# Routing each token tile beside the output projection, and the second layer's modulation ahead of its use

## The chip, the cores and the metric

The kernel runs on one core of one Trainium2 chip. The metric is the device time of one execution, in microseconds (us). The kernel before took 2386.52 us as the median of three runs (2384.01 to 2393.23).

## The reference

Two layers over 512 latent and 256 context tokens of width 1024, all in float32. The first layer mixes tokens with gated DeltaNet and grouped attention heads, the second with neighbourhood attention; each layer ends in an expert-choice mixture of 16 experts. What matters here is the end of each layer:

```python
h = h + mod_l[2] * y_lat                       # y_lat = heads @ w_out
h = h + mod_l[5] * expert_choice_ffn(modulate(h, ln2_g[layer], mod_l[3], mod_l[4]), *moe)
# modulate(x, g, shift, scale) = rms_norm(x, g) * (1 + scale) + shift
def expert_choice_ffn(h, w_router, w_gate, w_up, w_down):
    cap = max(1, EC_CAPACITY * t // N_EXPERTS)
    aff = jax.nn.softmax((h @ w_router).astype(F32), axis=-1)
    gate, idx = lax.top_k(jnp.swapaxes(aff, 1, 2), cap)
    xs = jax.vmap(lambda hb, ib: hb[ib])(h, idx)
    hid = silu(xs @ w_gate) * (xs @ w_up)
    y = (hid @ w_down) * gate                  # scattered back to the tokens and added
```

Each of the 16 experts picks its 64 best latent tokens (and 32 context tokens in the first layer, where the context goes through the same weights). The choice needs the logits of all tokens; so nothing of an expert can start before the last tile of the output projection has been normalised and multiplied by the router.

## The kernel before, in words

Tokens lie in tiles of 128: two of context, four of latents. Each engine runs a program of its own, written out by hand; semaphores join them, and every engine takes its instructions in the written order. The stages around the change are these.

- **Output projection** (outproj0_pe in the first layer, outproj_pe in the second; outproj_dve on VectorE). TensorE makes one half tile (128 tokens by 512 columns) after the other, 8 blocks of weights each; a half has the number j, two halves are a tile. VectorE multiplies half j with the modulation's gate (L1838) while it adds half j-1 to the residual stream H (L1846). Four PSUM banks let TensorE run four halves ahead. Of the first four halves of the first layer, half of the products are made earlier. The first layer has 12 halves, the second 8.
- **Second normalisation and router** (norm_act, norm_dve, norm_pe, logits_pe, pick_pe, pick_dve). ScalarE squares each tile of H as it is finished and takes one root over all; VectorE scales all tiles (L378); TensorE turns them (L403), VectorE and ScalarE modulate what was turned (L390, L364), TensorE multiplies with the router (L1912) and turns back (L1929), VectorE sums four groups (L1974) and takes the maximum (L1975), the softmax, and eight rounds of max / find / replace. The last small steps copy the token numbers out of PSUM (L2018, TOKL; L2021, TOKC; L2031), and GpSimd gathers the tokens of the first pair of experts (L2328, L2330); TensorE turns them (L2138, L2142), VectorE and ScalarE modulate (L2244, L2218).
- **Experts** (moe_pe and others). Pairs of experts, 24 MB of weights to a pair, streamed by SyncE into 8 or 12 slots that are full before the first pair starts; each slot is loaded again when its products are done.
- **Between the layers** the last pair's sums go back to the tokens (last_back, L2165, with the additions L2262), then TensorE turns the second layer's modulation rows (ada_finish_pe, L256), spreads the gates (ada_gates_pe, L279, copied by ScalarE L287), and the first normalisation of the second layer follows.

The order of work is the order of the code.

## Time and profile before

| what | value |
|---|---|
| median of the runs | 2386.52 us (2384.01 to 2393.23) |
| the profiled execution, first to last instruction | 2382.3 us |
| TensorE busy | 2112.3 us, 89% |
| VectorE busy | 762.8 us, 32% |
| ScalarE busy | 447.2 us, 19% |
| mean granted TensorE clock | 0.935 |

Shares are averages over stages that have different limits. The profile's busy time of TensorE holds modelled ends of pipelined matmuls; a float32 matmul shows as two records, a transpose as one. The chain of waits follows the work that ended last back through the program; a difference in a stage that is not on it is worth nothing.

### The profile page before, as it was taken

What the parts mean: (1) busy time and instruction counts of PE and PEld (TensorE: products, weight loads), DVE (VectorE), ACT (ScalarE), POOL (GpSimd) and SP (SyncE); (2) the same over time, 40 slices, a digit from 0 to 9 for tenths busy, and PEclk for the clock granted to TensorE, in tenths of its full rate; (3) what the DMA queues carried; (4) which work ended last, traced back from release to release, by engine and by line L of the source; (5) the groups of instructions that cost most, each with busy time, mean ns of one, the idle gap of its engine ahead of it and who ended that gap; (6) DMA issues with size and microseconds to landing.
All of it is one profiled execution on the core that took longest, in us unless ns stands there. A gap on an engine that the chain in (4) does not pass through costs nothing.

```text
span 2382.3 us, 32937 instructions
## 1 busy us (share of the span) xinstructions
PE 2112.3 (89%) x13760; PEld 1076.7 (45%) x13760; DVE 762.8 (32%) x1384; ACT 447.2 (19%) x1008; POOL 121.9 (5%) x119
## 2 busy tenths in 40 slices
PE   5998999818689849999999989999999399999997
PEld 3544666517685413333333334554674144444442
DVE  2143523588874341011011113000681511111113
ACT  2213421575321110000000012000561000000001
POOL 0000000030110000011111000000000000000000
PEclk9999999857679969999999999999999699999999
DMA  7219730132125339999999982210313399999996
GB/s 285 71 64 345 248 130 13 38 95 84 63 77 200 113 126 378 398 395 399 390 398 395 401 343 77 60 44 1 111 41 134 132 408 421 421 421 421 421 421 276
DMA packets 110618, 551.30 MB, mean 231 GB/s; under 512 B 13024, under 2 KB 25824, under 8 KB 61328
## 3 DMA queue, kind: packets, MB, share of 16 engines
q1 hardware_dynamic: 102512, 522.29, 55.6%
q0 software_dynamic: 7168, 23.83, 3.5%
q10 hardware_dynamic: 800, 3.15, 0.3%
q8 instruction: 111, 1.82, 0.3%
q14 instruction: 27, 0.22, 0.0%
HBM read 525.27 MB, written 22.38 MB: 230 GB/s over the span
## 4 chain that ended last, share of the span: by engine, by line
PE 75%; DMA 11%; DVE 9%; ACT 2%; issue 2%; SPq 0%; POOL 0%; DVEq 0%; POOLq 0%; ACTq 0%
PE ps L2104 22%; PE ps L2114 5%; DMA ring_sb<-expert_w_up 5%; PE ps L498 5%; PE ps L1789 3%; PE ps L901 3%; PE ps L2468 3%; PE ps L1821 2%; PE ps L2440 2%; PE ps L2449 2%; PE ps L2132 2%; DMA ring_sb<-ada_w 2%; PE ps L2151 2%; PE ps L900 2%; PE ps L244 2%
## 5 line engine op out<-in xcount | busy, mean ns | idle before, releaser
L2104 PE MATMUL ps<-work_sb 128*32 128x512 f32 (+1 forms) x2432 | 408.1, 593 | 9.6 <-ACT work_sb L2235 5.5
L2104 PE MATMUL ps<-ring_sb,work_sb 128*32 128x512 f32 (+1 forms) x2048 | 300.5, 599 | 16.6 <-DMA ring_sb<-expert_w_up 9.8
L2104 PEld LDWEIGHTS ps<-work_sb 128*32 128x32 f32 (+1 forms) x2432 | 123.0, 120 | 231.5 <-issue 224.2
L2104 PEld LDWEIGHTS ps<-ring_sb,work_sb 128*32 128x32 f32 (+1 forms) x2048 | 87.8, 118 | 204.3 <-issue 198.1
L2291 DVE TENSOR_TENSOR work_sb<-ps,work_sb 128x512 f32<-128x512 f32 x32 | 20.6, 687 | 437.1 <-PE ps L2114 329.8
L2225 ACT ACTIVATE work_sb<-ps 128x1024 f32<-128x1024 f32 x16 | 16.4, 1024 | 515.9 <-PE ps L2114 295.8
L498 PE MATMUL ps<-ring_sb,work_sb 128*128 128x512 f32 (+1 forms) x288 | 109.2, 541 | 0.9 <-DVE work_sb L390 0.9
L2114 PE MATMUL ps<-work_sb 128*32 128x512 f32 x768 | 100.7, 592 | 0.0
L2114 PE MATMUL ps<-ring_sb,work_sb 128*32 128x512 f32 x768 | 100.4, 593 | 0.0
L901 PE MATMUL ps<-work_sb,ring_sb 128*128 128x512 f32 x192 | 98.0, 592 | 0.0
L2310 DVE SCALAR_TENSOR_TENSOR work_sb<-ps,work_sb,gates_sb 128x1024 f32<-128x1024 f32 x16 | 20.5, 1284 | 232.9 <-PE ps L2114 124.8
L2235 ACT COPY work_sb<-ps 128x512 f32<-128x512 f32 x32 | 17.3, 589 | 405.7 <-PE ps L2192 405.7
L244 PE MATMUL ps<-ring_sb,sT_sb 128*32 128x512 f32 x384 | 57.0, 692 | 30.0 <-DMA ring_sb<-ada_w 28.2
L1789 PE MATMUL ps<-ring_sb,work_sb 128*128 128x512 f32 x192 | 82.8, 592 | 0.0
L498 PEld LDWEIGHTS ps<-ring_sb,work_sb 128*128 128x128 f32 x288 | 55.6, 194 | 52.4 <-issue 46.2
L2253 DVE TENSOR_TENSOR h_sb<-ps,h_sb 128x512 f32<-128x512 f32 x64 | 42.5, 688 | 100.2 <-PE ps L2151 100.2
L2468 PE MATMUL ps<-ring_sb,work_sb 128*128 128x512 f32 x160 | 68.8, 592 | 0.0
L2244 DVE TENSOR_SCALAR work_sb<-ps,scaleT_sb,modT_sb 128x128 f32<-128x128 f32 x128 | 42.2, 403 | 82.5 <-PE ps L2132 65.0
L2449 PE MATMUL ps<-work_sb,ring_sb 128*128 128x512 f32 x128 | 65.4, 592 | 0.0
L784 DVE TENSOR_REDUCE work_sb<-ps 128x1 f32<-128x768 f32 (+1 forms) x48 | 35.2, 775 | 78.5 <-PE ps L708 78.5
L2151 PE MATMUL ps<-work_sb 128*128 128x512 f32 x128 | 58.9, 604 | 1.5 <-DVE work_sb L2310 1.5
L2104 PE MATMUL ps<-h_sb,work_sb 128*64 128x512 f32 x128 | 57.6, 592 | 0.6 <-DMA work_sb<-expert_w_down 0.6
(405 smaller groups left out, 2913.2 us busy)
## 6 DMA issues: line engine op xcount, KB each, us to landing
work_sb<-expert_w_down SPq DMA_DIRECT2D x88, 1024.0 KB, 17.4
work_sb<-expert_w_gate SPq DMA_DIRECT2D x64, 1024.0 KB, 9.5
ring_sb<-expert_w_gate SPq DMA_DIRECT2D x64, 1024.0 KB, 10.0
ring_sb<-expert_w_up SPq DMA_DIRECT2D x64, 1024.0 KB, 13.9
work_sb<-expert_w_up SPq DMA_DIRECT2D x56, 1024.0 KB, 14.6
...
```

The source lines that it names most:

```text
L244: mm = pe.matmul(ps[32 * q:32 * q + 32, bank, :], sT[:, k, :], w[:, a * 512:(a + 1) * 512], start=(k == 0), stop=(k == KT - 1))
L498: mm = pe.matmul(ps[:, j % 4, 0:N], A[:, k, tok_cols(tt):tok_cols(tt) + P], w[:, (k % 2) * N:(k % 2 + 1) * N], start=(k == 0), stop=(k == ...
L900: pe.matmul(ps[:, b + 1, 0:CTX], w[:, k, :], A[:, k, 0:CTX], start=(k == 0), stop=(k == KT - 1))
L901: mm = pe.matmul(ps[:, b, :], w[:, k, :], A[:, k, LO:LO + LAT], start=(k == 0), stop=(k == KT - 1))
L1789: mm = pe.matmul(ps[:, EVEN_BANKS[j % 4], :], YT[:, tt, k, :], w[:, half * 512:half * 512 + 512], start=(k == 0), stop=(k == KT - 1))
L1821: mm = pe.matmul(ps[:, 4 + j % 4, :], c(k), w[:, half * 512:half * 512 + 512], start=(k == 0), stop=(k == KT - 1))
L2104: mm = pe.matmul(ps[g:g + wide, bank + n, :], lat_src[:, k, g:g + wide], us[e][:, n * 512:(n + 1) * 512], start=(k == 0), stop=(k == KT - 1))
L2114: mm = pe.matmul(ps[g:g + 32, bank_c, :], ctx_src(k, e), us[e][:, n * 512:(n + 1) * 512], start=(k == 0), stop=(k == KT - 1))
L2132: mm = pe.matmul(ps[:, k // 4, k % 4 * P:(k % 4 + 1) * P], XM[:, CT + j, cols(k)], TAKE[:, p % 2, j, :], start=(j == 0), stop=(j == LT - 1))
L2151: pe.matmul(ps[:, 4 + g % 4, :], ONEHOT[:, j * P:(j + 1) * P], YL[l][:, half * 512:half * 512 + 512], start=True, stop=True).then_inc(h_mm, 1)
L2449: mm = pe.matmul(ps[:, b, :], w[:, k, :], AO[:, k, LO:LO + LAT], start=(k == 0), stop=(k == KT - 1))
L2468: mm = pe.matmul(ps[:, 2 * (i % 2) + side, :], AO[:, k, v_cols(m):v_cols(m) + P], w, start=(k == 0), stop=(k == KT - 1))
```

## The change

- The router no longer works on normalised tiles. A raw tile of H is turned as soon as it is added up (route_turn_pe), copied out of PSUM in two halves by VectorE (route_dve) and ScalarE (route_act), and multiplied by router weights that hold the modulation's scale (WRM, router_weights_dve); the root of the tile and the product of shift and router (CVEC) come in afterwards (route_logits_dve). Each tile's steps are written between the halves of the output projection (route_beside_pe); route_end_pe has what is left.
- VectorE adds half j right behind its multiplication, where before it added half j-1.
- The second layer's modulation is turned after half 1 of the first layer's output projection; its gates are spread during the first layer's choice of tokens; only two gates are made instead of four. The tables of both layers are kept.
- The first normalisation of the second layer goes tile by tile between the last additions of the experts' sums (norm_row_dve).
- Normalised rows are stored tile by tile; the first gather waits for TOKL alone, the second (context) for TOKC, and the first products for half of the modulated tokens.
- GpSimd loads SEL1 and the router's weights (WR) right behind the late half of H (x); in the second layer WR goes ahead of the final gain.

On TensorE, first layer, from the first four half products on, before; L1789 are products of the output projection (8 to a half), L1761 turns of the heads' output, L403 turns of the normalised tiles:

```order
L1789 MATMUL ps<-ring_sb,work_sb 128x512 x16
L1761 MATMUL ps<-base_sb,h_sb 128x128 x16
L1789 MATMUL ps<-ring_sb,work_sb 128x512 x80
L403 MATMUL ps<-base_sb,work_sb 128x128 x36
L1912 MATMUL ps<-work_sb 32x512 x4
L1912 MATMUL ps<-work_sb 32x256 x4
```

and now, from half 2 on; L1798 is the projection, L1898 the turn of a raw tile, L1916 the spread of the shift's product, L1931 the logits of a tile, L1937 their turn back:

```order
L1798 MATMUL ps<-ring_sb,work_sb 128x512 x4
L1898 MATMUL ps<-base_sb,h_sb 128x128 x8
L1798 MATMUL ps<-ring_sb,work_sb 128x512 x4
L1916 MATMUL ps<-work_sb,base_sb 128x16 x2
L1931 MATMUL ps<-work_sb 32x128 x8
L1798 MATMUL ps<-ring_sb,work_sb 128x512 x8
L1937 MATMUL ps<-base_sb,work_sb 128x128
L1898 MATMUL ps<-base_sb,h_sb 128x128 x8
L1798 MATMUL ps<-ring_sb,work_sb 128x512 x8
L1931 MATMUL ps<-work_sb 32x128 x8
L1798 MATMUL ps<-ring_sb,work_sb 128x512 x8
```

Behind every odd half from 3 on now stand the logits of a tile, behind every even half from 4 on a turn back and the turn of the next tile.

On VectorE, same place, halves 6 and 7, with the semaphores that each instruction waits for; L1851 is the gate's multiplication, L1857 the addition, L2016 and L2005 copies out of PSUM, L2023 the sum of groups, L2007 and L2009 the inverse root and the normalised tile:

```order
L1851 TENSOR_TENSOR work_sb<-ps,gates_sb 128x512 [waits op_mm]
L1857 TENSOR_TENSOR h_sb<-h_sb,work_sb 128x512 [waits h_late,op_ok]
L2016 COPY work_sb<-ps 128x128 [waits rl_mm]
L1851 TENSOR_TENSOR work_sb<-ps,gates_sb 128x512 [waits op_mm]
L1857 TENSOR_TENSOR h_sb<-h_sb,work_sb 128x512 [waits h_late,op_ok]
L2023 TENSOR_REDUCE work_sb<-ps 128x16 [waits rl_mm]
L2025 SCALAR_TENSOR_TENSOR work_sb<-work_sb,stats_sb 128x16 [waits lg_ok]
L2005 COPY work_sb<-ps 128x512 [waits rl_mm,rt_mm]
L2007 RECIPROCAL stats_sb<-stats_sb 128x1 [waits rt_ok]
L2009 TENSOR_SCALAR work_sb<-h_sb,stats_sb 128x1024 [waits rc_ok]
```

The copies that TensorE's new instructions need stand behind the multiplication and the addition of the same half; before, only L1838 and L1846 stood here.

The diff, cut to its core:

```diff
                 else:
                     pe.wait_ge(op_ok, j - 3)
                     half_products(j, turned + list(range(4, KT)))
+                route_beside_pe(pe, 0, j)
+            route_end_pe(pe, 0)
...
-        def outproj_dve(dve, u0, tiles, mm_sem, prod_sem, ok_sem, w, PROD, base=0, banks=(4, 5, 6, 7)):
+                route_beside_pe(pe, 1, j)
+            route_end_pe(pe, 1)
+
+        def outproj_dve(dve, l, u0, mm_sem, prod_sem, ok_sem, PROD, banks=(4, 5, 6, 7)):
+            tiles, base = routed_tiles(l), OP0 * l
...
+            for j in range(n):
+                tt, half = tiles[j // 2], j % 2
+                if j < n - 1:
+                    dve.wait_ge(mm_sem, max(base - 1, 0) + j + 1)
+                else:
+                    dve.wait_ge(w_free, u0 + KT)
+                v = 1 if tt < CT else 0
+                nc.vector.tensor_tensor(PROD[:, j % 4, :], ps[:, banks[j % 4], :], gate_at(l, 0, v)[:, half * 512:half * 512 + 512],
+                                        ALU.mult).then_inc(ok_sem, 1)
+                dve.wait_ge(ok_sem, base + j + 1)
+                if l == 0:
+                    dve.wait_ge(h_back if tt < CT else h_late, 16)
+                hh = H[:, tt, half * 512:half * 512 + 512]
+                nc.vector.tensor_tensor(hh, hh, PROD[:, j % 4, :], ALU.add).then_inc(prod_sem, 1)
+                if j == 1 and l == 0:
+                    ada_finish_dve(dve, 1, (0, 1))
+                if j == 2:
+                    router_weights_dve(dve, l)
+                if j % 2 == 0 and j >= 4:
+                    route_sums_dve(dve, l, j // 2 - 2)
+                if j % 2 == 1 and j >= 5:
+                    route_logits_dve(dve, l, (j - 5) // 2)
+                if j % 2 == 1 and j >= 3:
+                    route_dve(dve, l, (j - 3) // 2)
+            last = len(tiles) - 1
+            route_sums_dve(dve, l, last - 1)
+            route_dve(dve, l, last)
+            route_logits_dve(dve, l, last - 1)
+            route_sums_dve(dve, l, last)
+            route_logits_dve(dve, l, last)
...
+        def route_turn_pe(pe, l, n):
+
+            tt = routed_tiles(l)[n]
+            pe.wait_ge(op_x, OP0 * l + 2 * n + 2)
+            if n == 0 and l == 0:
+                pe.wait_ge(modT_ok, 5)
+            if n > 0:
+                pe.wait_ge(rt_dve, NT * l + n)
+                pe.wait_ge(rt_act, NT * l + n)
+            for k in range(KT):
+                tr = pe.transpose(ps[:, TURN_BANKS[l][k // 4], k % 4 * P:(k % 4 + 1) * P], H[:, tt, cols(k)], IDENT)
+                if k % 4 == 3:
+                    tr.then_inc(rt_mm, 1)
+
+        def route_shift_pe(pe, l):
+
+            if l == 0:
+                pe.wait_ge(yt_ok, NT)
+            pe.wait_ge(mo["wr"], 16 * (l + 1))
+            pe.wait_ge(modT_ok, MODULATED["n2_%d" % l])
+            for k in range(KT):
+                mm = pe.matmul(ps[0:2, LOGIT_BANK[l], P:P + NE], MOD[:, l, :, 3, k], WR[:, k, :], start=(k == 0), stop=(k == KT - 1))
+            mm.then_inc(rl_mm, 1)
+
...
+        def route_logits_pe(pe, l, n):
+
+            tt = routed_tiles(l)[n]
+            if n > 0:
+                pe.wait_ge(rl_ok, logits_ok(l, 2 * n + 1))
+            for half in range(2):
+                pe.wait_ge((rt_dve, rt_act)[half], NT * l + n + 1)
+                for j in range(4):
+                    k = 4 * half + j
+                    w = WRM[:, 1 if tt < CT else 0, k, :]
+                    w = bass.AP(w.tensor, w.offset, [w.ap[0], [1, 32]])
+                    mm = pe.matmul(ps[32 * j:32 * j + 32, LOGIT_BANK[l], 0:P], w, RT[:, k, :], start=(half == 0), stop=(half == 1))
+            mm.then_inc(rl_mm, 1)
+
+        def route_back_pe(pe, l, n):
+
+            pe.wait_ge(rl_ok, logits_ok(l, 2 * n + 3))
+            pe.transpose(ps[:, BACK_BANK[l], 0:P], TURNED, IDENT).then_inc(rl_mm, 1)
...
+        def route_beside_pe(pe, l, j):
+
+            if j == 1:
+                route_shift_pe(pe, l)
+                if l == 0:
+                    ada_finish_pe(pe, 1, (0, 1))
+            if j >= 4 and j % 2 == 0:
+                route_back_pe(pe, l, j // 2 - 2)
+            if j >= 2 and j % 2 == 0:
+                route_turn_pe(pe, l, j // 2 - 1)
+            if j == 3:
+                route_spread_pe(pe, l)
+            if j >= 3 and j % 2 == 1:
+                route_logits_pe(pe, l, (j - 3) // 2)
+
+        def route_end_pe(pe, l):
+            last = len(routed_tiles(l)) - 1
+            route_back_pe(pe, l, last - 1)
+            route_turn_pe(pe, l, last)
+            route_logits_pe(pe, l, last)
+            route_back_pe(pe, l, last)
+
+        def route_act(act, l):
+            root_table(act)
+            for n, tt in enumerate(routed_tiles(l)):
+                act.wait_ge(op_x, OP0 * l + 2 * n + 2)
+                if n >= 2:
+                    act.wait_ge(sq_ok, tiles_before(l) + n - 1)
+                nc.scalar.activation(MJ[:, n % 2, :], H[:, tt, :], ACT.Square, accum_out=stat_t[:, tt:tt + 1]).then_inc(sq_ok, 1)
+                act.wait_ge(rt_mm, 2 * (NT * l + n) + 2)
+                if n > 0:
+                    act.wait_ge(rl_mm, logits_mm(l, 2 * n + 1))
+                nc.scalar.copy(RT[:, 4:8, :].rearrange("p k t -> p (k t)"), ps[:, TURN_BANKS[l][1], :]).then_inc(rt_act, 1)
+                act.wait_ge(sq_ok, tiles_before(l) + n + 1)
+                nc.scalar.activation(stat_t[:, 8 + tt:9 + tt], stat_t[:, tt:tt + 1], ACT.Sqrt, bias=EPSC, scale=1.0 / D) \
+                    .then_inc(rt_ok, 1)
+
...
+        def route_dve(dve, l, n):
+
+            tt = routed_tiles(l)[n]
+            dve.wait_ge(rt_mm, 2 * (NT * l + n) + 1)
+            if n > 0:
+                dve.wait_ge(rl_mm, logits_mm(l, 2 * n + 1))
+            nc.vector.tensor_copy(RT[:, 0:4, :].rearrange("p k t -> p (k t)"), ps[:, TURN_BANKS[l][0], :]).then_inc(rt_dve, 1)
+            dve.wait_ge(rt_ok, tile_roots_before(l) + n + 1)
+            nc.vector.reciprocal(stat_t[:, 16 + tt:17 + tt], stat_t[:, 8 + tt:9 + tt]).then_inc(rc_ok, 1)
+            dve.wait_ge(rc_ok, tile_roots_before(l) + n + 1)
+            nc.vector.tensor_scalar(XM[:, tt, :], H[:, tt, :], stat_t[:, 16 + tt:17 + tt], None, ALU.mult).then_inc(xn_ok, 1)
+
+        def route_sums_dve(dve, l, n):
+
+            dve.wait_ge(rl_mm, logits_mm(l, 2 * n + 3))
+            if n == 0:
+                nc.vector.tensor_copy(CVEC.rearrange("p v e -> p (v e)"), ps[:, BACK_BANK[l], P:P + 2 * NE]).then_inc(rl_ok, 1)
+            nc.vector.tensor_copy(TURNED, ps[:, LOGIT_BANK[l], 0:P]).then_inc(rl_ok, 1)
+
+        def route_logits_dve(dve, l, n):
+
+            tt = routed_tiles(l)[n]
+            dve.wait_ge(rl_mm, logits_mm(l, 2 * n + 4))
+            groups = ps[:, BACK_BANK[l], 0:P].rearrange("p (j e) -> p e j", j=4)[:, 0:NE, :]
+            nc.vector.tensor_reduce(LG[:, tt, :], groups, AX, ALU.add).then_inc(lg_ok, 1)
+            dve.wait_ge(lg_ok, NT * l + n + 1)
+            nc.vector.scalar_tensor_tensor(AFF[:, tt, :], LG[:, tt, :], stat_t[:, 16 + tt:17 + tt],
+                                           CVEC[:, 1 if tt < CT else 0, :], ALU.mult, ALU.add).then_inc(rl_ok, 1)
...
             tr.then_inc(mo["aft"], 1)
+            if l == 0:
+                ada_gates_pe(pe, 1)
             pe.wait_ge(mo["sid"], 2 * l + 2)
             n = C0 + NE if l == 0 else NE
...
             for e in range(2):
                 r = slice(CAP_L * e, CAP_L * e + CAP_L)
+                last = nc.vector.tensor_copy(TOKL[r, :], ps[r, 4, e:NE:2])
+            last.then_inc(mo["sg"], 1)
+            if l == 0:
+                for e in range(2):
+                    r = slice(CAP_C * e, CAP_C * e + CAP_C)
+                    last = nc.vector.tensor_copy(TOKC[r, :], ps[r, 4, C0 + e:C0 + NE:2])
+                last.then_inc(mo["sg"], 1)
+            for e in range(2):
+                r = slice(CAP_L * e, CAP_L * e + CAP_L)
                 if l == 1:
...
                     if l == 0:
+                        if m == 0 and k == 0:
+                            pe.wait_ge(mp["xsc"], p + 1)
                         if m == 2 and k == 0:
...
-                    last = nc.vector.tensor_scalar(XP[:, k, :], ps[:, k // 4, k % 4 * P:(k % 4 + 1) * P],
-                                                   AT[:, 1, 0, k:k + 1], modT[:, 0, 3, k:k + 1], ALU.mult, ALU.add)
-                last.then_inc(mp["xs"], 1)
+                    last = nc.vector.tensor_scalar(XP[:, k, :], ps[:, TOKEN_BANK[l] + k // 4, k % 4 * P:(k % 4 + 1) * P],
+                                                   SCALE[:, l, 1, 0, k:k + 1], MOD[:, l, 0, 3, k:k + 1], ALU.mult, ALU.add)
+                    if k % 4 == 3:
+                        last.then_inc(mp["xs"], 1)
...
                     hh = H[:, tt, half * 512:half * 512 + 512]
                     nc.vector.tensor_tensor(hh, ps[:, BACK_BANKS[g % 4], :], hh, ALU.add).then_inc(h_add, 1)
+                    if half == 1 and g >= 3:
+                        norm_row_dve(dve, "n1_1", g // 2 - 1, LATENTS_FIRST[g // 2 - 1], XNO)
 
...
             def gather(p):
                 pool.indirect_dma_start(XG, None, xm_rows, at(TOKL[:, p:p + 1])).then_inc(mp["got"], 16)
                 if l == 0:
-                    pool.indirect_dma_start(XGC[0:64], None, xm_rows, at(TOKC[0:64, p:p + 1])).then_inc(mp["got"], 16)
+                    if p == 0:
+                        pool.wait_ge(mo["sg"], 2)
+                    pool.indirect_dma_start(XGC[0:64], None, xm_rows, at(TOKC[0:64, p:p + 1])).then_inc(mp["gotc"], 16)
...
             pool.dma_start(H[:, CT:NT, :], t["x"].rearrange("(t p) d -> p t d", p=P)).then_inc(h_late, 16)
-            pool.wait_ge(gate_ok, 4)
-            pool.wait_ge(w_free, U_MOE[0])
+            pool.wait_ge(dn_ok, len(ORDER))
+            pool.dma_start(SEL1, t["sel"].rearrange("p (s m) -> p s m", s=8)).then_inc(ada1_in, 16)
             pool.dma_start(WR, t["router"][0].rearrange("p (k e) -> p k e", k=KT)).then_inc(mo["wr"], 16)
             moe_pool(pool, 0)
             odd_pool(pool)
             pool.wait_ge(op_mm, OP0)
+            pool.dma_start(WR, t["router"][1].rearrange("p (k e) -> p k e", k=KT)).then_inc(mo["wr"], 16)
             pool.dma_start(FING, t["fin_g"].partition_broadcast(P)).then_inc(fin_in, 16)
-            pool.dma_start(WR, t["router"][1].rearrange("p (k e) -> p k e", k=KT)).then_inc(mo["wr"], 16)
             moe_pool(pool, 1)
```

## Rows read from the trace of the kernel before

**Rows 1.** Page, part 4: the chain that ended last, by engine.
```profile
PE 75%; DMA 11%; DVE 9%; ACT 2%; issue 2%; SPq 0%; POOL 0%; DVEq 0%; POOLq 0%; ACTq 0%
```
**Rows 2.** Chain in order of time: start us, us, what.
```profile
749.37 68.68 PE ps L1789 x160
...
867.59 5.87 DMA work_sb<-xm_rows,work_sb
...
1889.80 4.35 DMA work_sb<-xm_rows,work_sb
```
**Rows 3.** Timeline, VectorE: start us, us, engine line operation, count [idle before <-releaser].
```profile
818.08 0.69 DVE L1838 TENSOR_TENSOR work_sb<-ps,gates_sb 128x512 f32<-128x512 f32 x1 [5.58 <-PE ps L1789]
818.69 1.70 DVE L1846 TENSOR_TENSOR h_sb<-h_sb,work_sb 128x512 f32<-128x512 f32 x2
...
841.20 0.25 DVE L1975 TENSOR_REDUCE work_sb<-work_sb 128x6 f32<-128x96 f32 x1
...
863.72 0.15 DVE L2018 CAST work_sb<-ps 64x8 uint32<-64x8 f32 x1
...
865.25 0.17 DVE L2031 TENSOR_SCALAR work_sb<-ps 64x16 uint32<-64x16 f32 x1
875.59 2.64 DVE L2244 TENSOR_SCALAR work_sb<-ps,scaleT_sb,modT_sb 128x128 f32<-128x128 f32 x8 [10.18 <-PE ps L2138]
...
1437.32 3.40 DVE L378 TENSOR_SCALAR work_sb<-h_sb,stats_sb 128x1024 f32<-128x1024 f32 x5
1441.56 0.75 DVE L378 TENSOR_SCALAR work_sb<-h_sb,stats_sb 128x1024 f32<-128x1024 f32 x1 [0.84 <-PE ps L279]
...
1867.80 0.22 DVE L1975 TENSOR_REDUCE work_sb<-work_sb 128x4 f32<-128x64 f32 x1
```
**Rows 4.** Groups of instructions by form, VectorE: a copy of 128 columns out of PSUM.
```profile
L535 DVE COPY work_sb<-ps 128x128 f32<-128x128 f32 x6 | 1.8, 292 | 20.7 <-PE ps L498 20.7
```
**Rows 5.** Timeline, TensorE, several stretches.
```profile
112.33 0.59 PE L593 MATMUL ps<-work_sb 128*128 128x8 f32 x4
112.77 0.37 PE L594 MATMUL ps<-work_sb,base_sb 128*128 128x16 f32 x2
...
747.46 1.91 PE L1761 MATMUL ps<-base_sb,h_sb 128*128 128x128 f32 x16
...
833.57 1.50 PE L1912 MATMUL ps<-work_sb 128*32 128x512 f32 x16
...
879.31 3.64 PE L2104 MATMUL ps<-ring_sb,work_sb 128*32 128x512 f32 x16 [2.61 <-issue]
...
1421.30 12.23 PE L2165 MATMUL ps<-work_sb 128*128 128x512 f32 x24 [2.24 <-DVE work_sb L2316]
...
1442.37 1.70 PE L403 MATMUL ps<-base_sb,work_sb 128*128 128x128 f32 x12 [0.85 <-DVE work_sb L378]
...
1794.12 55.20 PE L1821 MATMUL ps<-ring_sb,work_sb 128*128 128x512 f32 x128 [1.73 <-DVE work_sb L2588]
```
**Rows 6.** Timeline, GpSimd: its DMA issues.
```profile
749.68 0.78 POOL L2872 DMA_DIRECT2D h_sb<-x  x1 [18.16 <-PE ps L1761]
...
866.25 1.04 POOL L2328 DMA_INDIRECT work_sb<-xm_rows,work_sb  x1 [44.05 <-DVE work_sb L2031]
```
**Rows 7.** DMA issues: count, KB each, median us from issue to landing.
```profile
h_sb<-x POOLq DMA_DIRECT2D x1, 2048.0 KB, 8.7
```
**Rows 8.** Timeline, ScalarE.
```profile
820.42 1.06 ACT L351 ACTIVATE work_sb<-h_sb 128x1024 f32<-128x1024 f32 x1 [6.73 <-DVE h_sb L1846]
...
876.73 2.48 ACT L2218 ACTIVATE work_sb<-ps,modT_sb,scaleT_sb 128x64 f32<-128x64 f32 x8 [12.42 <-PE ps L2142]
```
**Rows 9.** Windows: stretch, us, PE, PEld, DVE, ACT, POOL busy (count), clock, DMA share, GB/s.
```profile
1419.00:1421.00 2.00, 0.07 (x4) 0.00 (x0) 1.78 (x2) 0.00 (x0) 0.00 (x0) 1.00 0.52 80
1422.00:1424.00 2.00, 2.00 (x4) 0.75 (x3) 0.69 (x1) 0.00 (x0) 0.00 (x0) 0.60 1.00 393
1794.00:1796.00 2.00, 1.89 (x5) 0.93 (x6) 0.06 (x1) 0.51 (x2) 0.00 (x0) 1.00 0.00 0
```

297 lines of the change are left out of this document (131 added, 166 removed).

## The prediction

> **What bounds the kernel now.** I read the chain of waits first: 75% of it is TensorE, 11% DMA, 9% VectorE [rows 1]. So a microsecond of TensorE's stream in a stage that is on the chain is a microsecond of the kernel. The chain in order of time then says which stages those are: in the first layer's output projection it is TensorE alone for 68.68 us, without one piece of another engine between, up to 818.05 [rows 2]. The timeline of VectorE says what it does meanwhile: it waits 5.58 us of every half for TensorE, and its own multiplication and addition are 0.69 and 0.68 us [rows 3]. The reader is to see here that VectorE has room in the projection, TensorE has none. Behind the projection it is turned round: the maximum over the logits starts at 841.20, 23.15 us after the last product, and in the second layer at 1867.80, 18.5 us after 1794.12 + 55.20 = 1849.3 [rows 3, 5]. These two tails are what the change can shorten. The choice of tokens that follows (841.20 to 863.6) is untouched.
>
> **Part 1: the tails.** What is left behind the last half, e being the moment at which VectorE sees it done: multiplication and addition 1.4 us [rows 3]; group sum and combination of the tile before, 0.2 each (near the 0.25 of a small reduce [rows 3]), and the copy of 512 columns (0.7, as long as the multiplication): e + 2.45. Logits on TensorE to e + 3.6, the copy of 128 columns 0.29 [rows 4], the turn back, the last tile's turn (8 of 1.91 / 16 = 0.12, with latency 1.2): e + 5.4. ScalarE's copy and root on the last tile, beginning behind that turn, end at e + 6.4, its square (1.06 [rows 8]) is long done. Inverse and normalised tile on VectorE (0.2 + 0.68), which stand ahead of the sums: e + 7.35. Two sums, a combination, one copy and a turn back: e + 8.8. So the maximum starts 8.8 us behind the last half in place of 23.15 and 18.5: **-14.3 and -9.7 us**. ScalarE's change of tables for the exponential comes behind its last root and is hidden by VectorE's 2.4 us there; bare it would be another 1.3.
>
> **Part 2: what is put between the halves.** The order of the changed program decides this one. Behind odd half j TensorE has the logits of a tile, and they wait for a copy that VectorE makes only after multiplying and adding half j itself. Behind an even half TensorE has a turn back, which waits for a copy that again follows the multiplication and the addition of the same half. VectorE cannot begin these before TensorE has finished the half, and behind TensorE's waiting instruction stand the 8 products of the next half, which wait with it. The four banks ahead are worth nothing then. Price of a wait: odd, 1.4 + 0.4 + 0.7 = 2.45 us (2.05 for j = 3, where no sums stand ahead), even, 1.4 + 0.29 = 1.7 us. A restart adds 0.16: a product occupies 0.43 (68.68 / 160) and its end is seen after 0.59, so one overlap is lost.
>
> TensorE's own work: a turn of a tile 1.0 (8 x 0.12 [rows 5]), a turn back 0.15. The logits of a tile are 8 float32 matmuls, 16 records; with the same weights and longer rows 16 (L1912) took 1.50 us [rows 5], by columns alone they would be 0.4. I take 1.0, keep 0.4 and 1.6. The product of shift and router is 16 records of tiny matmuls, at (112.77 - 112.33) / 4 = 0.11 [rows 5] 1.8 us; its weights are two columns wide, I take 1.5, keep 1.0 and 1.8. The turn of the modulation rows, 8 turns, is 1.0.
>
> One more wait, first layer only: the product of shift and router needs WR. GpSimd issues the load of H at 749.68, which lands 8.7 us later, at 758.4 [rows 6, 7]; SEL1 (512 KB) and WR (64 KB) are issued behind it on the same queue. At the rate of that load (2048 KB in 8.7) they need up to 2.4 more, at the engines' full rate 1.4: WR lands near 760. Half 1 is done at 818.05 less eight halves of 6.87 and two of 3.43, that is 756.2. Wait 3.8 us; keep 0 (WR overtakes) and 5.
>
> First layer, halves 1 to 10: WR 3.8 + 1.5 + 1.0; turn 1.0; j = 3: 2.05 + 0.16 + 1.0 = 3.2; j = 5, 7, 9: 3.6 each, 10.8; j = 4, 6, 8, 10: 1.7 + 0.16 + 0.15 + 1.0 = 3.0 each, 12.0. Sum **+33.3**. Second layer (WR is loaded a whole half earlier), halves 1 to 6: 1.5 + 1.0 + 3.2 + 3.6 + 2 x 3.0 = **+15.3**.
>
> **Part 3: the first gather.** Only TOKL is awaited now: two copies of 0.15 from 863.6 on, in place of everything up to 865.42 [rows 3]; GpSimd's issue moves from 866.25 to 864.7. A lone gather took 4.35 us from its issue in the second layer; in the first two of them and SEL1 took from 866.25 to 867.59 + 5.87 = 873.5 [rows 2, 6]. The latents' tokens now don't wait for the context's: landed by 869.2, turned by 871.2, half modulated (half of 2.64 [rows 3]) by 872.6, where the first product of experts came at 879.31 [rows 5]. The context's tokens, ready at about 875.7 with ScalarE's 2.48 [rows 8], are needed after the latents' first products, 3.64 us at that clock. **-6.3**, keep -4 and -7. In the second layer one reordered copy, **-0.5**.
>
> **Part 4: between the layers.** Before, the last normalised tile was done at 1442.3, for its last scale waited for the gates' products (L378) [rows 3]. Now VectorE has 12 additions of 0.69, six inverses and scales of 0.2 + 0.68 and small zeroings of about 1 us: some 14.6 us from about 1422.5 (1421.30 [rows 5] and a slow first product), plus 1.5 in the slow start, 1438.6. TensorE has then been idle for 5 us and turns the first columns slowly, 0.5. **-3.2**, keep -1 and -5. Two copies of gates and eight records of gate products move under the 22 us of the token choice, where TensorE and ScalarE wait anyway; without that cover they would be 3.4 us.
>
> **Part 5: TensorE's clock.** After 2.24 us of idleness [rows 5] the granted clock fell from 1.00 to 0.60 of the next two microseconds, between 2.4 and 1.2 GHz [rows 9]; after 1.73 idle at the start of the second projection it stayed at 1.00 [rows 5, 9]. The long waits here are 2.45, followed by thin logits, the short ones 1.7. In the first case 24 products took 12.23 where 24 x 0.43 = 10.3 would do, about 1.7 more (VectorE's additions share in that). I take such a fall for half of the six odd waits, none for the even: **+5**, keep 0 and 20.
>
> The Trainium skill, "TensorE: Matmul & The Clock Gate", section "HAM oscillation — how this bites in real kernels", has the clock fall only after idleness longer than any wait counted here; by it this term is 0 and the sum 5 us less. Row 9's fall after 2.24 us disagrees, so the row goes into the sum.
>
> **The sum.** 33.3 - 14.3 - 6.3 = +12.7 in the first layer; -3.2 between; 15.3 - 9.7 - 0.5 = +5.1 in the second; clock +5: +19.6 us. A late start of the experts passes on whole: their slots are full before they start in both kernels and are refilled only as they are used. The profiled execution spans 2382.3 us, 4.2 less than the runs' median of 2386.5; so 2382.3 + 19.6 + 4.2 = **2406 us**. Its own range, by the bounds above, is 2395 to 2421.
>
> **Rivals.**
> - *The hand-overs cost nothing* (faster). If VectorE's copies were always ready when TensorE asks, 12 waits with restarts (26.0), the wait for WR (3.8) and the clock's 5 go: 2406 - 34.8 = 2371. For it speaks that VectorE is idle for 5.58 us of each half; against it, that this idleness lies before the end of the half, and the copies are written behind it. It decides from the point where the 12 waits, 2.2 us on average with their restarts, fall to 0.95: then the clock stays up too (-5), and the other 14.6 us of the sum are gone. Chance 0.07.
> - *Part of it is cheaper*: logits at 0.4, WR in time, no fall of the clock: 2406 - 3.6 - 3.8 - 5 = 2394, no difference that can be told. Chance 0.2.
> - *The clock falls at nearly every wait*: nine more falls of 1.7 us: 2421. For it, the thin matmuls behind each wait; against it, the even waits' length, which cost nothing before the second projection. Chance 0.15.
> - *The change doesn't reach the end*: the weight stream absorbs the late starts. DMA is 11% of the chain. Then only the transition is left, 2383. Against it, that the stream itself stands still until products free its slots. Chance 0.05.
> - The forecast: 0.5. Mishaps of no name, 0.03.
>
> Within 0.5% (11.9 us) a measurement of this kernel can hardly tell a difference; so faster is below 2374.6, slower above 2398.5. Faster 0.07, same 0.22 (the second rival, the fourth, and a little of the forecast's low end), slower 0.71. The range that leaves out 2 in 10 is 2387 to 2422.
>
> **What would show it.** In the changed profile: TensorE waits for VectorE's copy at L2005 behind odd halves, 2.0 to 2.5 us each, and for the copy at L2016 behind even ones, 1.5 to 1.9; the first projection's products end 33 us later after their start than before, the second's 15; the maximum (L2115) starts 8 to 10 us behind the last product; a wait of 3 to 5 us for WR at L1909 in the first layer only; the first expert products about 10 us after the chosen tokens are turned. If the waits at L1931 and L1937 are below 1 us, the step on hand-overs is wrong, and with it the sign.

## The result and the profile after

The changed kernel takes 2404.8 us as the median of four runs (2401.48 to 2411.64), the kernel before 2387.06 in four runs on the same chip (2384.01 to 2393.23). The ratio is 1.0085, with a 95% interval of 1.0062 to 1.0109: slower by 0.85%. The profiled execution spans 2399.7 us, 17.4 more than that of before; its mean granted clock is the same 0.935. One of the runs below, the sixth of the second experiment, took 3191.03 us at a mean granted clock of 0.659, a slower state of the chip, and is left out of that experiment's median. The page's chain by engine hardly differs from that of before [rows 1], so it can't say where the time went:

```profile
PE 74%; DMA 11%; DVE 10%; ACT 2%; issue 2%; SPq 1%; POOL 0%; DVEq 0%; POOLq 0%; ACTq 0%
```

The stages can. Their bounds are starts of TensorE's groups in the two timelines, except the end of each projection, which is the start of the next group less the wait printed for it.

| stage | before | after | difference |
|---|---|---|---|
| up to the second loop of the first projection | 749.37 | 744.52 | -4.9 |
| first projection to its last product | 68.7 | 104.6 | **+35.9** |
| to the first product of the experts | 61.3 | 40.7 | **-20.6** |
| experts, to the first product of the last sums | 542.0 | 545.5 | +3.5 |
| between the layers, to the mixer's first product | 31.3 | 26.5 | **-4.8** |
| the second layer's mixer | 341.5 | 340.6 | -0.9 |
| second projection | 55.2 | 70.8 | **+15.6** |
| to the first product of its experts | 49.7 | 39.7 | **-10.0** |
| to the end | 483.3 | 486.9 | +3.5 |

The difference of the first stage is not the change's: it took 744.2 to 749.8 us in ten profiles of changed kernels (this one and nine below) and 748.4 in a second profile of the kernel before. In the first projection the products of the halves used to run without a gap [rows 2]. Now TensorE's timeline (start us, us, engine line operation, count, and in brackets how long the engine was idle before and whom it waited for) reads so:

```profile
755.06 0.59 PE L1909 MATMUL ps<-work_sb,modT_sb 128*2 128x16 f32 x16 [3.51 <-issue]
755.58 1.98 PE L256 MATMUL ps<-base_sb,modrows_sb 128*128 128x128 f32 x8
...
765.63 0.61 PE L1916 MATMUL ps<-work_sb,base_sb 2*128 2x16 f32 x4
767.81 0.65 PE L1931 MATMUL ps<-work_sb 128*32 128x128 f32 x16 [1.57 <-DVE work_sb L2005]
768.39 8.77 PE L1798 MATMUL ps<-ring_sb,work_sb 128*128 128x512 f32 x16
778.98 0.33 PE L1937 MATMUL ps<-base_sb,work_sb 128*128 128x128 f32 x1 [1.81 <-DVE work_sb L2016]
...
780.11 7.03 PE L1798 MATMUL ps<-ring_sb,work_sb 128*128 128x512 f32 x16
789.75 0.65 PE L1931 MATMUL ps<-work_sb 128*32 128x128 f32 x16 [2.61 <-DVE work_sb L2005]
790.32 7.13 PE L1798 MATMUL ps<-ring_sb,work_sb 128*128 128x512 f32 x16
...
830.14 1.08 PE L1931 MATMUL ps<-work_sb 128*32 128x128 f32 x16 [2.61 <-DVE work_sb L2005]
831.15 8.12 PE L1798 MATMUL ps<-ring_sb,work_sb 128*128 128x512 f32 x16
...
851.75 0.65 PE L1931 MATMUL ps<-work_sb 128*32 128x128 f32 x16 [2.61 <-DVE work_sb L2005]
852.80 0.33 PE L1937 MATMUL ps<-base_sb,work_sb 128*128 128x128 f32 x1 [0.40 <-DVE work_sb L2016]
...
854.50 1.20 PE L1931 MATMUL ps<-work_sb 128*32 128x128 f32 x16
```

L1931 are the logits of a tile, L1937 is the turn back of the logits' sums, L1798 a half (7.03 us are its 8 products, 16 records, at full clock; 8.77 and 8.12 are halves that began at the lower one), L1898 the turn of a raw tile. All the waits are there that the prediction named. VectorE's timeline at 787 to 790 shows who is waited for:

```profile
787.18 0.69 DVE L1851 TENSOR_TENSOR work_sb<-ps,gates_sb 128x512 f32<-128x512 f32 x1 [8.26 <-PE ps L1798]
787.90 0.69 DVE L1857 TENSOR_TENSOR h_sb<-h_sb,work_sb 128x512 f32<-128x512 f32 x1
788.51 0.22 DVE L2023 TENSOR_REDUCE work_sb<-ps 128x16 f32<-128x64 f32 x1
788.77 0.24 DVE L2025 SCALAR_TENSOR_TENSOR work_sb<-work_sb,stats_sb 128x16 f32<-128x16 f32 x1
788.92 0.69 DVE L2005 COPY work_sb<-ps 128x512 f32<-128x512 f32 x1
```

VectorE idled 8.26 us until the half was done; the copy L2005 that TensorE waits for is the fifth instruction in its queue behind that moment, and ends at 789.61, 0.14 us before TensorE goes on. The idleness of VectorE is real, and it lies on the wrong side of the additions.

The tails are short now. The maximum over the logits, L2115, which stood at 841.20 and 1867.80 before [rows 3]:

```profile
1881.92 0.22 DVE L2115 TENSOR_REDUCE work_sb<-work_sb 128x4 f32<-128x64 f32 x1
```

In the first layer it starts at 857.88, 8.7 us behind the last product (849.14); here 8.75 behind 1873.17.

### The profile page after: what moved, and what is told of

Its sections match the earlier page's. It is cut to its first block, busy times and chain, and to the rows that moved or that the text cites. A ratio compares the mean times of both kernels' runs of the same rounds, so it can differ in the third digit from the quotient of the medians.

```text
span 2399.7 us, 33292 instructions
## 1 busy us (share of the span) xinstructions
PE 2119.6 (88%) x13904; PEld 1077.9 (45%) x13904; DVE 765.0 (32%) x1425; ACT 449.1 (19%) x1020; POOL 121.2 (5%) x119
## 3 DMA queue, kind: packets, MB, share of 16 engines
q1 hardware_dynamic: 102512, 522.29, 55.2%
## 4 chain that ended last, share of the span: by engine, by line
PE 74%; DMA 11%; DVE 10%; ACT 2%; issue 2%; SPq 1%; POOL 0%; DVEq 0%; POOLq 0%; ACTq 0%
PE ps L2258 22%; PE ps L2270 5%; PE ps L508 4%; DMA ring_sb<-expert_w_up 4%; PE ps L1798 4%; PE ps L911 3%; DMA work_sb<-expert_w_up 3%; PE ps L2628 3%; PE ps L1832 2%; PE ps L2600 2%; PE ps L2609 2%; PE ps L2288 2%; DMA ring_sb<-ada_w 2%; PE ps L2308 2%; PE ps L910 2%
## 5 line engine op out<-in xcount | busy, mean ns | idle before, releaser
L2449 DVE TENSOR_TENSOR work_sb<-ps,work_sb 128x512 f32<-128x512 f32 x32 | 20.6, 687 | 440.0 <-PE ps L2270 331.0
L1798 PE MATMUL ps<-ring_sb,work_sb 128*128 128x512 f32 x192 | 89.6, 621 | 0.0
L2628 PE MATMUL ps<-ring_sb,work_sb 128*128 128x512 f32 x160 | 68.8, 592 | 0.0
L1832 PE MATMUL ps<-ring_sb,work_sb 128*128 128x512 f32 x128 | 57.5, 603 | 1.7 <-DVE work_sb L2748 1.7
```

The source lines that it names most:

```text
L1798: mm = pe.matmul(ps[:, EVEN_BANKS[j % 4], :], YT[:, tt, k, :], w[:, half * 512:half * 512 + 512], start=(k == 0), stop=(k == KT - 1))
L1832: mm = pe.matmul(ps[:, 4 + j % 4, :], c(k), w[:, half * 512:half * 512 + 512], start=(k == 0), stop=(k == KT - 1))
L2628: mm = pe.matmul(ps[:, 2 * (i % 2) + side, :], AO[:, k, v_cols(m):v_cols(m) + P], w, start=(k == 0), stop=(k == KT - 1))
```

## The experiments

Ten runs follow: eight edits of the changed kernel, and the kernel before and the changed one once more. Line numbers in a fence are those of the kernel that it shows; an edit moves some of them by up to 8.

**VectorE's router work ahead of the additions.** VectorE's part of the router beside half j is issued at the top of the turn of the loop instead of its end; what it reads has been ready since the half before.

```diff
             for j in range(n):
                 tt, half = tiles[j // 2], j % 2
+                if j % 2 == 0 and j >= 4:
+                    route_sums_dve(dve, l, j // 2 - 2)
+                if j % 2 == 1 and j >= 5:
+                    route_logits_dve(dve, l, (j - 5) // 2)
+                if j % 2 == 1 and j >= 3:
+                    route_dve(dve, l, (j - 3) // 2)
                 if j < n - 1:
                     dve.wait_ge(mm_sem, max(base - 1, 0) + j + 1)
...
-                if j % 2 == 0 and j >= 4:
-                    route_sums_dve(dve, l, j // 2 - 2)
...
```

> The changed kernel, with VectorE's work for the router (both copies and the scaling of a tile) issued ahead of the two additions of its half instead of behind them; TensorE's order is untouched. Theory A (what the added work costs is mostly TensorE waiting for copies that stand behind the additions of the half that has just ended): inside the loop the waits ahead of L1931 (1.57 and three of 2.61 us in the first layer, 1.57 and 2.61 in the second) and ahead of L1937 (1.81 and three of 1.71; 1.81 and 1.71) go to under 0.3 us each, 16.3 + 7.7 us; the halves that ran at the lower clock after them (8.77, 8.12 and 8.09 instead of 7.03 us) give back some 4 us; each tail gets 1.5 us shorter. First projection 104.5 to about 85 us, second 70.8 to about 62 us, whole kernel about 2374 us, 0.987 of the changed kernel and some 0.5% below the kernel before. Theory B (TensorE's own added instructions are the price, the waits only show where VectorE is full): the copies now delay the additions, TensorE waits for product banks instead, and the time stays at 2400 to 2408. Theory C (the waits go, but TensorE's lower clock comes at other places): about 2385.

Measured: 2364.76 us (2361.42 to 2370.43), ratio to the kernel before 0.9918 (0.9897 to 0.9939). That is 40 us less than the changed kernel, and faster than before. The first projection took 83.9 us (744.16 to 828.05), the second 61.0; the way to the first product of the experts took 38.0 and 37.5 us instead of 40.7 and 39.7. TensorE in the same place as above:

```profile
754.57 0.59 PE L1909 MATMUL ps<-work_sb,modT_sb 128*2 128x16 f32 x16 [3.37 <-issue]
...
756.87 4.04 PE L1798 MATMUL ps<-ring_sb,work_sb 128*128 128x512 f32 x8
...
765.75 0.65 PE L1931 MATMUL ps<-work_sb 128*32 128x128 f32 x16
766.33 7.13 PE L1798 MATMUL ps<-ring_sb,work_sb 128*128 128x512 f32 x16
773.30 0.27 PE L1937 MATMUL ps<-base_sb,work_sb 128*128 128x128 f32 x1
...
774.36 7.03 PE L1798 MATMUL ps<-ring_sb,work_sb 128*128 128x512 f32 x16
781.33 0.64 PE L1931 MATMUL ps<-work_sb 128*32 128x128 f32 x16
...
828.05 0.64 PE L1931 MATMUL ps<-work_sb 128*32 128x128 f32 x16
829.83 0.33 PE L1937 MATMUL ps<-base_sb,work_sb 128*128 128x128 f32 x1 [1.14 <-DVE work_sb L2016]
```

The wait for the router's weights (L1909, 3.37 us) and the slow clock behind it are still there, since this edit doesn't touch them. None of the waits ahead of L1931 and L1937 is left inside the loop, and every whole half is at 7.03 or 7.13. Theory A stands; B and C fall. The gain was 9 us more than its 31. Between the profiles it is 36.8 (2399.7 to 2362.9). The two projections and the ways behind them gave 35.4, some 4 more than expected: the ways got shorter by 2.7 and 2.2 us where 1.5 each stood, and a wait costs a little more than its printed length (third experiment). The last stage gave 3.7, which came by the clock (below), and the experts' stage took 2.7 back. The other 3 are the scatter of the medians.

**TensorE's router work in the middle of the next half**, with VectorE's order left alone:

```diff
+        AMID = lambda j: True
...
-                route_beside_pe(pe, 0, j)
...
+                half_products(j, blocks[:len(blocks) // 2])
+                if j >= 1 and AMID(j - 1):
+                    route_beside_pe(pe, 0, j - 1)
+                half_products(j, blocks[len(blocks) // 2:])
+                if not AMID(j) or j == 2 * NT - 1:
+                    route_beside_pe(pe, 0, j)
```

(and the same in outproj_pe for the second layer).

> The changed kernel, with TensorE's work for the router behind half j issued in the middle of half j+1 instead; VectorE's order is untouched. The copies then have about 3.5 us of products as cover. Theory A: all waits in the loop go (16.3 + 7.7 us), and the 3.51 us wait for the router's weights with its low clock (1.2 us) too, since its first reader comes half a half later; clock after the waits gives some 3.7 us; the tails stay at 8.7. About 2372 us. Theory B (own work): 2400 to 2408 us, as little is moved in all. Theory C (falls of the clock elsewhere): about 2383.

Measured: 2368.52 us as the median of five runs (2365.52 to 2374.82), ratio 0.9932 (0.9908 to 0.9956). First projection 81.1 us (749.82 to 830.92), second 61.1, the ways behind them 40.6 and 39.9. The same waits inside the loop go by the other engine's order (behind the last half, where no further products follow, the 2.6 us stay), so the price belongs to the place where the two queues meet and not to either engine's load. The wait for the router's weights fell from 3.51 to 1.72 us rather than to nothing.

**Only the odd halves' work of VectorE ahead of the additions** (the two lines with j % 2 == 0 stay at the end).

> As the first of this call, but only VectorE's work of the odd halves (copy of the turned tile L2005, scaling, sums) stands ahead of the additions; the copy L2016 of the even halves stays behind them. Theory A: the waits ahead of L1931 go (9.4 us in the first layer, 4.2 in the second), those ahead of L1937 (7.0 and 3.5 us) stay; since all falls of the clock inside the loop came after waits ahead of L1931, they go too (some 3.7 us), and both tails get 1.5 us shorter: about 2384 us. If the clock fell because of waits of any length, some falls come back after the 1.7 us waits: about 2387. Theory B: 2400 to 2408.

Measured: 2381.10 us, ratio 0.9979 (0.9961 to 0.9996). First projection 91.9 us (749.44 to 841.37), 12.7 less than the changed kernel; second 65.0, 5.8 less.

```profile
771.78 7.13 PE L1798 MATMUL ps<-ring_sb,work_sb 128*128 128x512 f32 x16
780.72 0.33 PE L1937 MATMUL ps<-base_sb,work_sb 128*128 128x128 f32 x1 [1.81 <-DVE work_sb L2016]
...
788.82 0.65 PE L1931 MATMUL ps<-work_sb 128*32 128x128 f32 x16
789.39 7.13 PE L1798 MATMUL ps<-ring_sb,work_sb 128*128 128x512 f32 x16
798.24 0.33 PE L1937 MATMUL ps<-base_sb,work_sb 128*128 128x128 f32 x1 [1.71 <-DVE work_sb L2016]
```

The waits ahead of L1937 are there to the hundredth, those ahead of L1931 gone, and no half behind either is slow (the one behind the wait for the router's weights is, 4.33 us for 4 of its products). From here to the first experiment the four even waits (6.9 us) bring the first projection another 8.0, the two of the second (3.5) another 4.0: each is worth its printed length and 0.25 us for the restart. For an odd wait the same comparison gives less: from the start of the half at 780.11 to that of L1931 the changed kernel takes 9.64 us and the first experiment 6.97 (774.36 to 781.33), so the 2.61 us cost 2.67.

**The router's weights loaded ahead of the late half of H.**

```diff
             pool.dma_start(H[:, 0:CT, :], t["ctx"].rearrange("(t p) d -> p t d", p=P)).then_inc(h_back, 16)
+            pool.wait_ge(dn_ok, len(ORDER))
+            pool.dma_start(WR, t["router"][0].rearrange("p (k e) -> p k e", k=KT)).then_inc(mo["wr"], 16)
             pool.wait_ge(yt_tr, NT)
             pool.dma_start(H[:, CT:NT, :], t["x"].rearrange("(t p) d -> p t d", p=P)).then_inc(h_late, 16)
-            pool.wait_ge(dn_ok, len(ORDER))
             pool.dma_start(SEL1, t["sel"].rearrange("p (s m) -> p s m", s=8)).then_inc(ada1_in, 16)
-            pool.dma_start(WR, t["router"][0].rearrange("p (k e) -> p k e", k=KT)).then_inc(mo["wr"], 16)
```

> The changed kernel, with the load of the router's weights issued ahead of the late load of H and the two small ones on GpSimd's queue, which moves it some 1.3 us earlier and ahead of the large load's data. Theory A (the 3.51 us wait ahead of L1909 is that load, queued behind the H load's transfer): the wait goes to under 0.5 us, L256's eight columns blocks behind it take 1.1 us instead of 1.98 and the next half-half 3.6 instead of 3.96: some 4.7 us less, about 2400 us. Rival (the load itself takes its 10 us from issue to landing wherever it stands): the wait falls by 1.3 us only, and the time by 1.3 us, which is less than can be measured.

Measured: 2396.43 us, ratio 1.0045 (1.0029 to 1.0061). L1909 follows the half without a wait:

```profile
747.69 7.03 PE L1798 MATMUL ps<-ring_sb,work_sb 128*128 128x512 f32 x16
754.65 0.56 PE L1909 MATMUL ps<-work_sb,modT_sb 128*2 128x16 f32 x16
755.14 1.23 PE L256 MATMUL ps<-base_sb,modrows_sb 128*128 128x128 f32 x8
756.20 3.60 PE L1798 MATMUL ps<-ring_sb,work_sb 128*128 128x512 f32 x8
```

The edit moved the load much further than the 1.3 us of the expectation, since it also stands ahead of the wait for the last turns (yt_tr). GpSimd's issues, in the changed kernel and in this one:

```profile
744.99 0.79 POOL L3018 DMA_DIRECT2D h_sb<-x  x1 [20.89 <-PE ps L1770]
...
746.30 0.56 POOL L3021 DMA_DIRECT2D work_sb<-router  x1
```

```profile
731.98 0.57 POOL L3018 DMA_DIRECT2D work_sb<-router  x1 [5.07 <-DVE h_sb L1524]
748.15 0.75 POOL L3020 DMA_DIRECT2D h_sb<-x  x1 [15.60 <-PE ps L1770]
```

With a lead of 16 us the wait would be gone by the rival too, so its absence decides nothing. What decides is the time from issue to landing: 8.7 us in the changed kernel, where 2048 and 512 KB had been issued just ahead, and 2.2 us here, where the load was alone. So the load doesn't take its 9 us by itself, and the rival falls by that. That it landed right before TensorE went on (746.30 + 8.7 = 755.0, L1909 at 755.06) shows who was waited for.

The first projection took 98.3 us (747.69 to 845.94), 6.4 less than in the changed kernel: 3.5 for the wait, 1.1 for the slow clock behind it (1.98 and 3.96 against 1.23 and 3.60), and 1.6 because the half behind L1931 of j = 3 ran at full clock here.

**Both edits together.**

> Both edits together: VectorE's router work ahead of the additions of its half, and the load of the router's weights ahead of the late load of H. Theory A (two separate prices that add up): the first alone gave 2364.8 us, the second 8 us below the changed kernel's median of which its trace bears out 4.9 (wait of 3.51 and slow clock behind it); together 2356 to 2360 us, and the first projection 83.9 - 4.8 = 79 us. Rival (with the wait gone, TensorE reaches the early halves sooner and meets VectorE's queue or the late load of H instead): a new wait of 1 to 4 us in the halves 2 to 4, and 2362 to 2366 us.

Measured: 2363.26 us, ratio 0.9908 (0.9881 to 0.9935). The first projection took 79.25 us (747.19 to 826.44), as theory A had it, with no wait in it. The whole kernel can't be told from the first experiment, though, and its median lies in the rival's range and not in the theory's 2356 to 2360; but the new wait that the rival needs is nowhere in the trace. This execution reached the projection 3.0 us later, and its experts' stage was 1.6 us longer. It is 0.9% faster than the kernel before and 1.7% faster than the changed one, and the version to keep.

**The second layer's first normalisation whole again**, behind all twelve additions, the modulation still early (norm_row_dve in last_added removed, norm_rows_dve over all tiles behind it, one root on ScalarE).

> The changed kernel, with the second layer's first normalisation done whole, behind the last of the twelve additions, as in the kernel before; the modulation stays early. From first product of the last sums to first product of the mixer the changed kernel takes 26.5 us, the one before 31.3. Theory A (the 4.8 us come mostly from the modulation, as VectorE has the same instructions either way and is kept waiting 0.17 us by each product): this stage takes 27.5 to 28.5 us, one to two more than the changed kernel, too little to be seen in the median. Rival (tile by tile is what brings them): the stage returns to 31 us.

Measured: 2406.19 us, ratio 1.0102 (1.0064 to 1.014). The stage took 28.6 us, 2.1 more than the 26.5 of the changed kernel. This comparison is clean, since the 12 products (24 records) of the last sums ran at the same clock in both; the two experiments on the gather show what those alone do. Each line is the start of the last sums in one kernel: the changed one, this one, that with the late gather, and the one with all waits around the gathers undone.

```profile
1435.33 10.54 PE L2322 MATMUL ps<-work_sb 128*128 128x512 f32 x24 [2.24 <-DVE work_sb L2474]
```

```profile
1439.74 10.54 PE L2322 MATMUL ps<-work_sb 128*128 128x512 f32 x24 [2.24 <-DVE work_sb L2472]
```

```profile
1437.32 12.23 PE L2324 MATMUL ps<-work_sb 128*128 128x512 f32 x24 [2.23 <-DVE work_sb L2476]
```

```profile
1448.38 12.23 PE L2326 MATMUL ps<-work_sb 128*128 128x512 f32 x24 [2.24 <-DVE work_sb L2478]
```

10.54 us at full clock, 12.23 where it fell, which is what the kernel before had in both of its profiles, and two of the ten profiles of changed kernels; whether the change has a part in that stays open. With the slow products the stage takes 28.4 and 28.5 us in the changed layout. So of the 4.8 us, 1.9 are the clock's, 2.1 come from going tile by tile, and 0.8 are left for the early modulation, as a remainder that no run tested. Theory and rival of the expectation are both wrong on who brings the gain; the number for the stage was missed by 0.1.

**The first gather late.** GpSimd waits for all tables, and TensorE turns the latents' tokens only when the context's are there.

```diff
             pool.wait_ge(mo["sg"], 2 * l + 1)
+            if l == 0:
+                pool.wait_ge(mo["sg_all"], 1)
...
                 pe.wait_ge(mp["got"], 16 * (NPAIR * l + p + 1))
+                if l == 0:
+                    pe.wait_ge(mp["gotc"], 16 * p + 16)
```

> The changed kernel, with the first gather issued only when all index tables are written, and TensorE's turning of the latents' tokens waiting for the context's tokens too, as before. Theory A: from the last turn of the choice (L2092) to the first product of the experts the changed kernel takes 9.8 us; here it takes 5 to 6.3 us more, and since a late start of the experts passes on whole, the kernel takes 5 to 6 us more, about 2410. Rival (the experts' stage is bound by the stream of weights, whose engines are busy for 1.0 of it, and would swallow a later start): the stage of the experts, 543 to 548 us in the changed kernels so far and 542 before, gets shorter by what the gather gets longer, and the time stays.

Measured: 2405.82 us, ratio 1.0099 (1.0063 to 1.0135). From L2092 to the first product 12.7 us against 9.8: 2.9 more, half of what was expected. The experts' stage took 544.0 us, 1.5 less than in the changed kernel, and the median is 1.0 us higher: whether the stage takes such a delay up, as the rival had it, is within the scatter and not shown.

**The kernel before, once more.**

> The kernel before, unchanged, for one more profile: is the 3.5 us by which the experts' stage of the first layer (542.0 us from first product to first product of the last sums) and that of the second (483.3 us to the end) got longer an effect of the change, or of the execution? If of the change: again 541 to 543 and 483 to 484 us here. If of the execution (rate of the weight stream, place of a slow clock): 543 to 547 us, as in the five traces of changed kernels (544.9 to 548.2).

Measured: 2381.23 us, one run. The experts' stage took 542.6 us (877.55 to 1420.19), the last one 483.9, the one between the layers 31.4. All three stay at the level of before; what that says is weighed below.

**All waits around the gathers as before.** Besides the two of the late gather, the first products wait for both halves of the modulated tokens and for the context's.

> The changed kernel, with all waits around the gathers as before: gather when all tables are written, TensorE turns the latents' tokens only when the context's are there too, products of a pair only when both are modulated. The experts' stage of the first layer took 542.0 and 542.6 us in two profiles of the kernel before, 544.0 in the changed kernel with the late gather, 544.9 to 549.8 in the other changed ones. If the waits between the pairs are what lets the weight stream run at 393 to 394 GB/s over the first 240 us of the stage (changed: 385 to 391): the stage is back at 542 to 543 us and the rate at 393. If they are not: 544 to 547 us and 388 to 391 GB/s, and the cause stays open. From the last turn of the choice to the first product: 14.3 to 14.7 us as before, against 9.8 in the changed kernel.

Measured: 2413.36 us, one run. From L2092 to the first product 15.0 us. So the 5.2 us of the gather come in two parts, 2.9 from the wait for the tables and the context's tokens, 2.2 from products that start on half of the tokens, each by one pair of profiles. But the experts' stage took 552.5 us, the longest of all, at 384 GB/s. So the missing waits between the pairs don't explain why the stage is longer in the changed kernel: with them back it was not shorter.

**The changed kernel, once more.**

> The changed kernel itself once more, for a second profile: how far the stages of one kernel differ between two executions. If the small differences between the kernels are real, the experts' stage is again 545 to 547 us, the stage between the layers 26.5, and the lower clock comes after some of the 2.61 us waits again, not always the same ones.

Measured: 2405.55 us, one run. Experts 546.3 us, between the layers 26.5. Where the clock fell differs from the first profile:

```profile
793.75 0.65 PE L1931 MATMUL ps<-work_sb 128*32 128x128 f32 x16 [2.61 <-DVE work_sb L2005]
794.33 7.13 PE L1798 MATMUL ps<-ring_sb,work_sb 128*128 128x512 f32 x16
...
813.95 1.08 PE L1931 MATMUL ps<-work_sb 128*32 128x128 f32 x16 [2.61 <-DVE work_sb L2005]
814.96 8.07 PE L1798 MATMUL ps<-ring_sb,work_sb 128*128 128x512 f32 x16
```

## Why the prediction was right

The forecast was 2406 us and "slower"; measured were 2404.8, and 17.4 us between the profiles where the sum said 19.6. Most terms held one by one. A few us of the agreement are luck: the stages that the sum prices gave 16.1 us, 3.5 less than it, and the others 1.3: -4.9 is scatter ahead of the changed stages, -0.9 the mixer's, and twice +3.5, in the experts' stage and the last one, had no term in the sum.

- **The step that decided it, the hand-overs.** Predicted were 2.45 us for an odd wait, 2.05 at j = 3 and 1.7 for an even one. Measured were 2.61, 1.57 and 1.71 to 1.81; with the restart an odd one cost 2.67 and an even one 1.96, where 2.61 and 1.86 stood. At j = 3 a product of TensorE's own (L1916, 0.61) stands ahead of the wait and uses up part of it, which the working left out. The two experiments on either engine's order took these waits away, the first with some 2.5 us of each tail, the second with half of the wait for WR, and the kernel became faster than before. The first rival's figure of 2371 for hand-overs that cost nothing came out as 2364.8 and 2368.5, by making the change so.
- **TensorE's own work** is the remainder, 79.25 - 68.68 = 10.6 us in the first projection and 61.0 - 55.2 = 5.8 in the second. The working had 12.1 and 6.8. Two terms were mis-sized: the logits of a tile, taken at 1.0, occupy 0.57 to the next start, and the product of shift and router, taken at 1.5, occupies 0.5. Both values had come from the nearest rows, which are of other shapes [rows 5]; for the logits the bound by columns alone, 0.4, was the nearer end, for the other even the low end of 1.0 was too high. Left out were the spread L1916 (0.54 to the next start) and 0.1 us for each half that something is put behind (6.97 us to the next start against 6.87), 1.0 in the first layer.
- **The wait for WR**: 3.51 us where 3.8 stood, for the reason given, as the fourth experiment showed.
- **The tails**: 8.7 and 8.75 us where 8.8 stood. Saved were 14.4 and 9.7.
- **The gather**: 6.2 us saved (16.15 to 9.96 from L2091's turn to the first product) where 6.3 stood. The working's own steps give 6.7 (879.31 - 872.6), so 0.4 were lost in it. The second profile of the kernel before has 15.3 in place of 16.15, so the size of the gain is known to about 1 us; two parts of it were tested, 2.9 and 2.2. In the second layer it was 0.4 where 0.5 stood.
- **Between the layers**: 4.8 where 3.2 stood. The mechanism gave 2.9, the other 1.9 were the clock's, which the working had slow in both kernels.
- **The clock.** Taken was a fall for half of the six odd waits in the loops. It fell behind three (768.39, 831.15 and, in the second layer, 1855.21), for 1.0 to 1.6 us each and 0.43 in the logits ahead of two of them. It also fell behind the wait for WR, 1.1, and in each tail, about 0.5: some 6.6 us in all against 5. The windows of the changed kernel show both outcomes behind one and the same wait of 2.61 us (the column behind POOL is the mean granted clock; 1.00 is 2.4 GHz, 0.50 is 1.2, and 0.64 a stretch that has both):

```profile
790.00:794.00 4.00, 4.00 (x25) 1.89 (x17) 0.46 (x1) 0.00 (x0) 0.00 (x0) 1.00 0.50 203
831.00:834.00 3.00, 3.00 (x10) 1.34 (x6) 0.00 (x0) 0.00 (x0) 0.00 (x0) 0.64 0.50 190
834.00:839.00 5.00, 5.00 (x13) 2.05 (x11) 0.00 (x0) 0.00 (x0) 0.00 (x0) 1.00 0.00 2
```

The rule that was weighed, "TensorE: Matmul & The Clock Gate" of the Trainium skill, section "HAM oscillation — how this bites in real kernels", would have had no fall behind any of the hand-overs. There the traces disagree, for the clock fell after waits of 1.57, 2.24 and 2.61 us. Only the wait for WR, 3.51 us, is long enough for it, and there they agree (though in the third experiment it fell behind 3.29 us too); the recorded sentence, which puts the whole term at 0 by this rule, passed over that wait, priced at 3.8. Of the rise at a kernel's start the page says in its section "Part 1: The HAM clock gate (the "warmup" mystery)" that its moment varies from run to run of one kernel. The traces show the like for the fall: two profiles of the changed kernel have it behind different halves (831.15 in the one, 814.96 in the other).

- **Experts, +3.5 us, not in the prediction.** "A late start of the experts passes on whole" holds nearly: the first experiment started them 23.8 us earlier and the last sums 21.1; whether the 2.7 us between are the early start's or scatter is open. In this stage the DMA engines are busy throughout and TensorE waits for them now and then (9.1 us in the changed kernel, 7.9 before), and the rate over 240 us, from 20 us behind the first product on, goes with its length (DMA share and GB/s are the last two columns; the kernel before in its second profile, the changed kernel, the kernel with all waits around the gathers undone):

```profile
897.55:1137.55 240.00, 237.62 (x2172) 1.00 1.00 394
```

```profile
909.80:1149.80 240.00, 235.44 (x2152) 1.00 1.00 389
```

```profile
915.90:1155.90 240.00, 232.32 (x2120) 1.00 1.00 384
```

1% of rate over such a stretch is 2.4 us. The stage took 542.0 and 542.6 in the kernel before and 544.0 to 552.5 in ten profiles of changed kernels, so the difference seems to belong to the change, though two profiles of before are few; which edit makes the stream slower stays open. The +3.5 of the last stage came by the clock: the stage took 483.3 and 483.9 before, and in the changed kernels five times 482.6 to 483.9 and five times 486.5 to 487.0. The difference lies in the first products of the second layer's experts. From the first of them to the 64 products that follow it takes 33.3 to 34.9 us in the seven short profiles and 37.3 to 37.8 in the five long ones, and the third ten microseconds read so, in the kernel before and in the changed one (the mean granted clock, third from the end, is 1.00 and 0.69):

```profile
1918.98:1928.98 10.00, 10.00 (x48) 3.41 (x50) 2.26 (x6) 0.00 (x0) 0.00 (x0) 1.00 1.01 422
```

```profile
1932.83:1942.83 10.00, 10.00 (x37) 3.94 (x38) 2.26 (x6) 0.00 (x0) 0.00 (x0) 0.69 0.99 383
```

The five long ones are those in which the clock also fell in the second layer's tail, where the logits of the last tile took 1.13 to 1.31 us instead of 0.70 or 0.71. They are among the seven profiles with a wait of 2.6 us ahead of the tail's first logits; of the other five profiles none is long. So the change seems to have opened the way to it, which no experiment tested by itself, and the sum had no term for it.

The rivals: "part of it is cheaper" was right on the logits and wrong on WR and the clock, which outweigh them; "the clock falls at nearly every wait" was wrong, as no half behind an even wait was slow and three of the six odd ones weren't either; "the change doesn't reach the end" was wrong, all stages passed their differences on but for the above.
